# Three stages of a two-block model kernel rearranged: the row load with its first products, the position-bias stage with the norm inside it, and the front of the attention projection

## The reference

```
x = first_block(x, ...)      # 2 layers: projections, dilated attention + retention mixers, gated conv FFN, norms
x = second_block(x, c_2, positions_2, rel_bias_2, ...):
  for i in range(2):
    sh1, sc1, g1, sh2, sc2, g2 = split(silu(c) @ ada_w[i] + ada_b[i], 6)
    h = modulate(rmsnorm(x, norm_g[i, 0]), sh1, sc1)
    y = conv_mixers(h, ...) if i == 0 else attn_mixers(h, positions, ..., rel_bias, ...)
    x = x + g1 * y
    h = modulate(rmsnorm(x, norm_g[i, 1]), sh2, sc2)
    x = x + g2 * hier_moe(h, ...)
  return rmsnorm(x, final_norm_g)
```

## Time and profile before

| | us |
|---|---|
| median of 3 runs | 3217.04 |
| lowest, highest | 3214.51, 3218.49 |
| profiled execution, its own time | 3213.69 |
| its span | 3211.9 |

### The profile page before, as it was taken

How to read it: one execution, slowest core, us unless ns; L and a number is a source line. 1 busy time by engine, 2 the same in 40 slices (tenths; PEclk the granted TensorE clock), 3 DMA queues, 4 the chain that set the end, 5 groups by cost and what they waited for, 6 DMA issues and landing times. The chain is left out here.

```text
span 3211.9 us, 40579 instructions
## 1 busy us (share of the span) xinstructions
PE 2958.0 (92%) x13962; PEld 2386.4 (74%) x13962; DVE 2446.5 (76%) x2669; ACT 1418.5 (44%) x1700; POOL 419.9 (13%) x247
## 2 busy tenths in 40 slices
PE   7998999999988999979979999995988979999995
PEld 6777788877777878757767888884765767888884
DVE  4566888565567996575978999996487769999996
ACT  1233211022323210164236777774336328777775
POOL 0110112211101113200000000001323100000001
PEclk9999999999989999979989999997999989999997
DMA  4242765333324663164239999994213349999994
GB/s 170 66 164 66 234 213 163 113 116 100 145 92 145 219 214 105 53 180 126 66 143 375 378 371 372 386 369 165 98 40 121 101 180 387 383 379 385 387 387 155
DMA packets 346602, 667.26 MB, mean 208 GB/s; under 512 B 21984, under 2 KB 138700, under 8 KB 338268
## 3 DMA queue, kind: packets, MB, share of 16 engines
q1 hardware_dynamic: 339708, 642.60, 56.9%
q0 software_dynamic: 6752, 22.81, 2.1%
HBM read 612.22 MB, written 53.13 MB: 207 GB/s over the span
## 5 line engine op out<-in xcount | busy, mean ns | idle before, releaser
L2936 DVE TENSOR_TENSOR expert_w_low<-expert_w_raw,expert_w_high 128x2048 fp32r<-128x2048 f32 x290 | 663.2, 2289 | 58.2 <-ACT expert_w_high L2892 57.9
L2892 ACT CAST expert_w_high<-expert_w_raw 128x2048 fp32r<-128x2048 f32 x290 | 554.8, 1915 | 197.5 <-PE bank L144 180.4
L142 PE MATMUL bank<-expert_w_high,expert_x_high 128*128 128x512 f32 x928 | 379.5, 409 | 6.7 <-DVE expert_w_low L2936 4.6
L142 PE MATMUL bank<-first_XH,first_w_high 128*128 128x512 f32 (+1 forms) x944 | 369.7, 392 | 0.2 <-DVE first_w_low L222 0.2
L144 PE MATMUL bank<-expert_w_high,expert_x_low 128*128 128x512 f32 x928 | 364.9, 393 | 0.0
L143 PE MATMUL bank<-expert_w_low,expert_x_high 128*128 128x512 f32 x928 | 363.8, 392 | 0.0
L143 PE MATMUL bank<-first_XL,first_w_high 128*128 128x512 f32 (+1 forms) x944 | 362.9, 384 | 0.0
L144 PE MATMUL bank<-first_XH,first_w_low 128*128 128x512 f32 (+1 forms) x944 | 362.6, 384 | 0.0
L222 DVE TENSOR_TENSOR first_w_low<-first_w_raw,first_w_high 128x2048 fp32r<-128x2048 f32 (+2 forms) x94 | 287.1, 3054 | 3.2
L220 DVE CAST first_w_high<-first_w_raw 128x2048 fp32r<-128x2048 f32 (+2 forms) x94 | 111.6, 1188 | 172.4 <-PE bank L144 151.5
L1440 ACT ACTIVATE ffn_conv<-bank,ffn_taps 128x512 f32<-128x512 f32 x88 | 68.4, 780 | 358.2 <-PE bank L144 358.2
(11 more groups left out here) (549 smaller groups left out, 5940.3 us busy)
## 6 DMA issues: line engine op xcount, KB each, us to landing
expert_w_raw<-in_moe_w_gate_dram SPq DMA_DIRECT2D x116, 1024.0 KB, 9.1
expert_w_raw<-in_moe_w_up_dram SPq DMA_DIRECT2D x116, 1024.0 KB, 12.7
expert_w_raw<-in_moe_w_down_dram SPq DMA_DIRECT2D x58, 1024.0 KB, 13.9
modulation<-in_moe_w_down_dram SPq DMA_DIRECT2D x58, 1024.0 KB, 14.0
ffn_mod_w<-in_ada_w_dram SPq DMA_DIRECT2D x48, 1024.0 KB, 5.0
first_w_raw<-in_w_up_dram SPq DMA_DIRECT2D x88, 512.0 KB, 6.4
first_w_raw<-in_w_down_dram SPq DMA_DIRECT2D x22, 1024.0 KB, 4.8
first_w_raw<-in_w_in_dram SPq DMA_DIRECT2D x20, 1024.0 KB, 5.0
```

What stands on the lines that cost most here:

```text
L142: nc.tensor.matmul(out, rounded(st[0]), rounded(mv[0]), start=start, stop=False)
L2892: nc.scalar.copy(rounded(high[:, part_of(e, n), :]), weights.place(place)).then_inc(w_high, 1)
L2936: nc.vector.tensor_tensor(rounded(low[:, part_of(e, n), :]), weights.place(place), high[:, part_of(e, n), :], ALU.subtract).then_inc(w_spl ...
```

## The change

In the load stage x comes as four DMAs of 512 KB with a semaphore each; weight slot 0 is issued behind the first, slot 1 last. PE turns tiles 0 to 2, makes the products of tile 0, turns tile 3, makes those of tiles 1 and 2, turns the c rows, makes those of tile 3. DVE splits both slots in this stage, slot 0 after tile 0's low parts. `project_phase` now skips slot 0's products always.

In the bias stage the stores' semaphores outlive the stage (`BiasStores`), the wait for them moves from its end to DVE's taps in the conv stage, and buffers are declared in another order. The norm's steps lie 13 pairs apart; all four shifts are DVE's and POOL has nothing left; signs cover three pairs of five (38 pairs, before 43; DVE's hits are 90, before 85); DVE's memset goes ahead of its wait for the positions.

In the attention projection values(0,1) comes before turn 1; ACT does a root on one column first, and splits slot 1 before it squares tile 1; DVE splits slot 1 before it scales tile 1, and takes tile 1's low parts before it adds tile 2.

```diff
...
-        x_loaded = ph.sem("x_loaded")
...
+        x_loaded = [ph.sem(f"x_loaded{t}") for t in range(TT)]
         X, ps, ident = G["X"], G["ps"], G["ident"]
+        C_BANK = 4
...
         def _(sp):
             sp.dma_start(ident, G["d"]["ident"][:, :]).then_inc(ident_loaded, 16)
-            sp.dma_start(X[:, :, :], G["d"]["x"][0].rearrange("(t p) n -> p t n", p=P)).then_inc(x_loaded, 16)
+            def load_rows(t):
+                sp.dma_start(X[:, t, :], G["d"]["x"][0, t * P:(t + 1) * P, :]).then_inc(x_loaded[t], 16)
+
+            load_rows(0)
+            first_weights.load(sp, 1)
+            for t in range(1, TT):
+                load_rows(t)
             sp.dma_start(c_rows[:, :], G["d"]["c_2"][:, :].rearrange("o (k p) -> (o k) p", p=P)).then_inc(c_loaded, 16)
             first_weights.load(sp, Weights.RING)
...
             nc.vector.memset(G["eps_norm"][:, :], NORM_EPS).then_inc(ones_set, 1)
-            for t in range(TT):
+            split.low_parts(dve, 0)
+            first_weights.split_slot(dve, 0)
+            for t in range(1, TT):
                 split.low_parts(dve, t)
+            first_weights.split_slot(dve, 1)
             dve.wait_ge(c_turned, 1)
-            nc.vector.tensor_copy(G["cond"][:, :], ps[0][:, 0:KD]).then_inc(c_copied, 1)
+            nc.vector.tensor_copy(G["cond"][:, :], ps[C_BANK][:, 0:KD]).then_inc(c_copied, 1)
 
         @block.tensor
         def _(pe):
-            pe.wait_ge(ident_loaded, 16)
-            pe.wait_ge(x_loaded, 16)
-            for t in range(TT):
+            def turn_rows(t):
+                pe.wait_ge(x_loaded[t], 16)
                 for j in range(2):
                     for i in range(4):
                         k = 4 * j + i
                         last = nc.tensor.transpose(ps[2 * t + j][:, i * P:(i + 1) * P], X[:, t, k * P:(k + 1) * P], ident)
                     last.then_inc(transposed, 1)
 
+            def products(t):
+                pe.wait_ge(split.low, 2 * t + 2)
+                return first_value_job(nc, G, first_weights, t)
+
+            pe.wait_ge(ident_loaded, 16)
+            for t in range(3):
+                turn_rows(t)
+            pe.wait_ge(first_weights.split, 1)
+            products(0)
+            turn_rows(3)
+            products(1)
+            products(2)
             pe.wait_ge(c_silu_done, 1)
-            pe.wait_ge(split.low, 1)
-            nc.tensor.transpose(ps[0][:, 0:KD], c_silu[:, :], ident[0:KD, 0:KD]).then_inc(c_turned, 1)
+            nc.tensor.transpose(ps[C_BANK][:, 0:KD], c_silu[:, :], ident[0:KD, 0:KD]).then_inc(c_turned, 1)
+            products(3).then_inc(first_weights.used, 1)
 
         @block.scalar
...
                     s = SLOTS * c + half
-                    if s == 0 and begun:
+                    if s == 0:
                         continue
...
             for s in range(len(weights.loads)):
-                if s >= Weights.RING or not begun:
+                if s >= Weights.RING:
...
         pa = ph.sb("p_a", [P, 4, PAD_A + SEQ])
+        cb = ph.sb("conv_b", [P, 4, SEQ])
+        diag = ph.sb("diagonal_taps", [P, PE_TAPS, P])
         ca = ph.sb("conv_a", [P, 4, SEQ])
-        cb = ph.sb("conv_b", [P, 4, SEQ])
         sq = ph.sb("squares", [P, 4, SEQ])
         std, rstd = sq[:, 0, :], sq[:, 1, :]
         total = sq[:, 0, :]
         part = sq
         ya_high_part = ph.sb("y_a_high", [P, 4, SEQ])
-        diag = ph.sb("diagonal_taps", [P, PE_TAPS, P])
+        ya_low_part = ph.sb("y_a_low", [P, 4, SEQ])
...
-        ya_low_part = ph.sb("y_a_low", [P, 4, SEQ])
...
                         bchain.link(V.scalar_tensor_tensor(cb[:, m, :], ub[:, m, w:w + SEQ], tap, cb[:, m, :], ALU.mult, ALU.add))
                     if m > 0 and w == own_taps(m) - 1:
+                        if m == 1:
+                            stores.wait(dve)
                         bchain.link(V.tensor_tensor(total[:, :], cb[:, 0, :] if m == 1 else total[:, :], cb[:, m, :], ALU.add))
                 taps_done = min(taps_done + count, ALL_TAPS)
...
-def bias_norm_phase(nc, G, g_dram, shift, scale, following, layer):
+class BiasStores:
+
+
+    PER, OUTS = 4, 3
+
+    def __init__(self, nc):
+        self.stored = [nc.alloc_semaphore(f"bias_rows_stored{s}") for s in range(self.OUTS)]
+        self.batches = [len(range(s, P // 2 // self.PER, self.OUTS)) for s in range(self.OUTS)]
+
+    def wait(self, eng):
+        for s in range(self.OUTS):
+            eng.wait_ge(self.stored[s], 32 * self.batches[s])
...
-    by_sign = [p % 3 != 2 for p in range(PAIRS)]
+    by_sign = [p % 5 % 2 == 0 for p in range(PAIRS)]
...
+        rows = ph.sb("rows", [P, TT, D])
+        gain = ph.sb("gain", [P, D])
         out = ph.sb("bias_rows", [P, OUTS, PER, SEQ])
-        gain = ph.sb("gain", [P, D])
...
-        stored = [ph.sem(f"stored{s}") for s in range(OUTS)]
+        stored = stores.stored
...
-        by_pool = ph.sem("shifted_by_pool")
-        by_dve = ph.sem("shifted_by_dve")
+        shifted = ph.sem("shifted")
...
-        SCALE_AT = {2 + t: t for t in range(TT)}
-        TURN_AT = {5 + 2 * t: t for t in range(TT)}
-        HIGH_AT = {7 + 2 * t: t for t in range(TT)}
-        LOW_AT = {8 + 2 * t: t for t in range(TT)}
-        WEIGHTS_AT = {24: 0, 34: 1}
+        GAIN_AT = 3
+        SCALE_AT = {4 + 13 * t: t for t in range(TT)}
+        TURN_AT = {8 + 13 * t: t for t in range(TT)}
+        HIGH_AT = {9 + 13 * t: t for t in range(TT)}
+        LOW_AT = {10 + 13 * t: t for t in range(TT)}
+        WEIGHTS_AT = {13: 0, 26: 1}
...
-            for s in range(OUTS):
-                sp.wait_ge(stored[s], 32 * len(range(s, PAIRS // PER, OUTS)))
...
-                if t % 2 == 1:
-                    dve.wait_ge(scaled, t + 1)
-                    dve.wait_ge(mod_loaded[1], 16)
-                    V.tensor_tensor(rows[:, t, :], rows[:, t, :], shift, ALU.add).then_inc(by_dve, 1)
-
+                dve.wait_ge(scaled, t + 1)
+                dve.wait_ge(mod_loaded[1], 16)
+                V.tensor_tensor(rows[:, t, :], rows[:, t, :], shift, ALU.add).then_inc(shifted, 1)
+
+            link(V.memset(wide[:, :, :], 0.0))
             dve.wait_ge(pos_loaded, 16)
             link(V.tensor_copy(pos[:, :], pos_i[:, :]))
-            link(V.memset(wide[:, :, :], 0.0))
...
-                if p == 1:
+                if p == GAIN_AT:
...
-        @block.gpsimd
-        def _(pool):
-            pool.wait_ge(mod_loaded[1], 16)
-            for t in range(0, TT, 2):
-                pool.wait_ge(scaled, t + 1)
-                nc.gpsimd.tensor_tensor(rows[:, t, :], rows[:, t, :], shift, ALU.add).then_inc(by_pool, 1)
-
...
-                pe.wait_ge(by_dve if t % 2 else by_pool, t // 2 + 1)
+                pe.wait_ge(shifted, t + 1)
...
             values(0, 0)
+            values(0, 1)
             turn_rows(1)
             values(1, 0)
-            values(0, 1)
             turn_rows(2)
...
 
+            nc.scalar.activation(first_root[:, :], G["eps_norm"][:, :], ACT.Sqrt)
             combine.weigh(act, 0)
             combine.square(act, 0)
             weights.split_high(act, 0, last_user)
             combine.weigh(act, 1)
             split.high_part(act, 0)
+            weights.split_high(act, 1, last_user)
             combine.square(act, 1)
-            weights.split_high(act, 1, last_user)
             combine.weigh(act, 2)
...
             combine.sum(dve, 1)
             combine.add(dve, 1)
+            weights.split_low_dve(dve, 1)
             scale_rows(1)
-            weights.split_low_dve(dve, 1)
             combine.sum(dve, 2)
+            split.low_parts(dve, 1)
             combine.add(dve, 2)
-            split.low_parts(dve, 1)
             combine.sum(dve, 3)
             scale_rows(2)
...
```

18 lines of the change are left out of this document (10 added, 8 removed).

## The result

The changed kernel takes 3200.7 us, the median of five runs (3198.0 to 3206.2), beside 3217.9 for the kernel before (3214.5 to 3220.4, five runs): a ratio of 0.995, with a 95% interval of 0.9936 to 0.9965, so 11 to 21 us less. The forecast was 3196.5 and a range of 3183 to 3208. It is faster by more than the 0.2% that can be told, and 4 us less so than forecast. The profiled execution has a span of 3198.9 us (3211.9 before), 13.0 less.

A forecast was written before the change was run, and what follows sets the result against it. PE, busy 92% of the span, was taken as the bound, so only its waits or slow running could be won. Gains of 9.1 + 3.7 + 4.7 + 3.0 = 20.5 us gave 3196.5 against the median 3217.0; range 3183 to 3208.

The forecast's parts named there:

- The walk: Position-bias pair loop, gone through step by step: the sum is 82.0 us, where it took 85.5, and the stage gains 3.7.
- (b): Position-bias pair loop: slow clock at the start, as in the projection, costs 2.2 us.
- (g): Position-bias pair loop: the clock falls around the two weight splits as it fell before, costing 2.0 us.
- (c): Position-bias pair loop: gain, scale and shift at pairs 3 and 4 leave PE waiting 0.8 us.
- (f): Position-bias pair loop: scales behind the two weight splits cost 1.2 us each, 2.4 in all.
- (d): Position-bias pair loop: four low parts, where DVE waits for ACT, cost PE 2.0 us each, 8.1 in all.
- (e): Position-bias pair loop: two weight splits three pairs behind a low part cost 2.3 us each, 4.6 in all.
- step (a): Position-bias pair loop: 64 pairs and four turns on PE take 61.9 us.
- Rival 1: Position-bias stage: the spread loop runs at PE's pace, up to 18 us more gain, 3178 to 3188; chance 0.14.
- Rival 2: Pair loop gives nothing and attention front only moves its wait: 14 us less, 3203 to 3209; chance 0.17.
- Rival 3: Position-bias loop: gaps throughout keep PE at 1.2 GHz, so the kernel is slower, 3231; chance 0.04.
- Rival 4: Load stage: the 1 MB slot delays x's tiles, products start near 16, gain 5.5 instead of 9.1, 3200; chance 0.07.

The follow-up runs named there:

- The shifted idle: Changed kernel with 20 more small turns of the index weights at 79.6 us of the attention projection stage, results unchanged; stage 209.2 us (210.9 in the changed kernel), ratio 0.9945.

## Why the prediction was right, and where it was wrong

**The load stage: right, -9.1 for -9.1.** Over the thirteen kernels that have it, slot 1's first product starts at 26.1 on average (25.3 to 26.8) in place of 35.28. The steps stand as worked out: tile 0 at 5.2 (5.4 forecast), products at 12.5 (12.7), DVE done at 22.7 (22). Weakest was the slot behind them: it was to land some 4 us after its issue and be split by 35, with 2 us to spare. It landed 7.1 us after its issue in the changed kernel's profile and was split at 37.9, 0.4 too late; elsewhere it took 5.0 to 6.5 us, and in the other twelve PE did not wait.

**The stores' wait: right, -4.7 for -4.7.** PE's idle behind the loop is 7.3 on average in the three kernels that wait (7.9, 7.1, 7.0), and 2.6 in the others. The start was to stay slow. In the changed kernel the first five products ran at 2.4 GHz and the next eight at 1.2. The stretch at the lower clock behind the first product is 3.4 us long, against 4.7 before, so little was won by it.

**The pair loop: right in sign, -1.8 for -3.7.** The walk gave 82.0 us and the changed loop took 84.0. Three steps were off, and two of them hid each other. The clock, steps (b) and (g), was to cost 2.2 + 2.0; but PE ran for 16.2 us at a granted 0.50, and 16.05 us of work at half pace cost 8.0, so 3.8 more than forecast. An idle of 2.2 us was taken for 2.2 us, and three of the five of over 2 us were followed by 3.3 to 3.4 us at the lower clock. The idles, steps (c) to (f), came to 12.5 us for 15.9: (d), the low parts, 2.37, 2.21, 2.19 and 2.21, 9.0 in all for 8.1; (e) and (f) 0.55, 2.05 and 0.89, 3.5 for 7.0; and none over 0.5 us for (c). That is 3.4 less, and it is luck that it nearly makes up for the clock. What is left of the loop, 84.0 - 12.5 - 8.0, is 63.5 us for 64 pairs and four turns at full pace, where step (a) had 61.9: 1.6 more.

The sign "DVE's low parts still waiting about 8 us" did not come: they waited 17.4. The prediction named the lockstep at the low parts as something that the change leaves in; the runs say how much that was: 11 us with the clock, by four pairs' distance in one line.

**The attention projection: wrong, +1.3 for -3.0.** With the old front the stage takes 209.2, 209.4 and 208.8, with the new one in seven kernels 210.4 on average (209.1 to 211.4). Two steps failed. The first is "turn 2 comes about 3.5 us earlier: -3.0". In the changed kernel it came 2.8 earlier, but a new idle (3.19 us) stands ahead of it, and turn 2 and the next products ran at 1.2 GHz. At slot 2's first product 1.2 us were left, 1.0 on average over the seven. That PE may meet it at 1.2 GHz was said and not priced. The second was not in the sum at all: what a shift of 1.2 us does to an idle 70 us later. The kernel before has that idle, and the clock held behind it; coming earlier, it cost 2.9 us in the changed kernel (1.2 to 2.9 in the eight kernels where the clock fell, 2.3 on average over the seven). The shifted idle showed, in one profile, that it is the time of the idle that decides it. That the early root is worth nothing was nearly right: turn 0 came 16.9 us into the stage on average with the new front, and 17.3 to 17.5 with the old, half a microsecond sooner.

**The sum.** -9.1 - 4.7 - 1.8 + 1.3 = -14.3 from the stages, where the forecast had -20.5: 1.9 us are missing in the loop and 4.3 in the attention stage. By the runs it is -16.1 (-11 to -21), so the forecast missed by 4.2 us; the 1.8 us between the stages and the runs are less than a ratio can tell. The total came inside the range because the two large terms were right by their own mechanisms. The clock has the largest share in what the two smaller ones lacked, but not all of it: in the loop it is partly made up for by shorter idles and joined by step (a), and in the attention stage 2.3 of the 4.3 us lie behind the later idle and 2.0 ahead of slot 2's first product.

**The rivals.** Rival 1 (the loop at PE's pace) needed the later low parts: with them the loop is 68.9 to 72.9. Rival 2 (the loop gives nothing, the front only moves its wait) came nearest in mechanism: loop -1.8, front +1.3. Its 14 us less would have been 3203. Its premise that DVE has 7 us more work does not hold: the added shifts and hits make 4.5 (2 x 1.23 + 5 x 0.41), and DVE was busy for 59.3 us of the changed loop and for 60.9 of the old one, where one scale took 3.40 us beside a shift of POOL. The front failed by PE's idle and the clock. Rival 3 had the right agent, the clock at intervals through the loop, and too high a price. Rival 4 did not occur.

## What to carry to other kernels

When an engine runs ahead of another by a ring of buffers, work that it gets back from the other belongs as many steps later in its list as it leads; placed by the order of the data, it costs the lead each time. Here moving one such piece by the lead took the loop from 84.0 to 72.9 us. Price an idle of PE with the clock behind it, and look which engine's chain ends the stage before a gain on PE is booked. A gain of a microsecond can be lost at an idle that nobody edited, so a change of under 5 us is judged from the stage's rows in several profiles.

## What the hardware showed that was not expected

- One and the same idle of PE, 2.7 us, left the clock at 2.4 GHz in four kernels and brought it down to 1.2 in eight, for 2.4 to 5.8 us. The Trainium skill (TensorE: Matmul & The Clock Gate, Why this matters for your kernels) tells kernels to avoid idles longer than this one. The trace is stricter: this one was enough when it came at the wrong time, and in the pair loop idles of 2.05 to 2.37 us were, three times of five.
- With 1.2 us of needless work on PE the stage was 1.7 us shorter (209.2 against 210.9, one profile each).
- The fall does not always come at the idle. In the kernel with splits moved the second idle ended 181.1 us into the stage, and PE ran at full pace until 182.6, then at half until 186.0.
- Stages without an edit differ by 3 to 4 us between profiles (from the conv stage's first product to the attention stage 731.4 to 735.4, the stages behind the chosen attention 662.3 to 665.5), as much as the two smaller terms of this change.
